# Stages of a two-block float32 network handed over token tile by token tile

## The chip, the cores and the metric

One core of a Trainium2 chip runs the whole program in one launch. The metric is device time in microseconds (us) from start to end, the median of several runs. The engines are TensorE (PE; its weight loads are listed as PEld), VectorE (DVE), ScalarE (ACT), GpSimd (POOL) and the queue engine SyncE (SP). Each engine works through its own instruction list in order and waits on semaphores that others raise.

## The reference

A first block (attention mixer and mixture of experts, two layers) feeds a second block, to which the change belongs. Its input x is 256 tokens by 1024 channels, float32, two layers deep:

```
for l in range(2):
    h = rms_norm(x, norm_pre[l, 0])
    x = x + 0.5 * rms_norm((silu(h @ w_gate) * (h @ w_up)) @ w_down, norm_post[l, 0])   # hidden width 2816
    h = rms_norm(x, norm_pre[l, 1])
    m = hybrid_mixer(h, ...)    # input product, three branches, merged = sum(gates * branch @ w_branch), m = merged @ w_out
    x = x + rms_norm(m, norm_post[l, 1])
    h = rms_norm(x, norm_pre[l, 2])
    x = x + 0.5 * rms_norm(swiglu_ffn(h, ...), norm_post[l, 2])
```

rms_norm divides each token's row by the root of its mean square over 1024 channels and multiplies by a gain row.

## The kernel before

Tokens lie on partitions in two tiles of 128 (`TT = 2`, index `tt`); `x` stays in SBUF. A product needs its left side transposed, so `h` is turned by PE in groups of four 128x128 blocks into one of two PSUM banks `t_bank` (`pe_xt`, L518). Float32 products are made from three matmuls (`mm3`, L477 to L479) of a high and a low part: ACT copies the transposed group into `xt_hi` (L525), DVE subtracts to get `xt_lo` (L533).

Weights stream through a ring of three units of 128x2048 numbers (`RING = 3`), worked in half units: SP loads a half into `w_raw`, ACT rounds it to `w_hi` (L461, `split_hi`), DVE makes `w_lo` (L466, `split_lo`), PE uses it for 12 matmuls and raises `w_used`. `ahead(u, k)` on ACT and DVE splits two halves that lie five halves (`AHEAD = 5`) in front. A half can be split only when PE has used the half six places earlier; that is what orders the splits on ACT and DVE between their other work. A unit of a 1024-wide product with 512 columns is 4 of the 8 contraction blocks, so a 512-column result takes two units and 48 matmuls for both token tiles.

A feed-forward (`feed_forward`) is 11 groups of 256 hidden columns: `gate_up` (two units into `s_bank`), SiLU on ACT (L1041), the product on DVE (L2011), the transposes of the hidden tile on PE (`hid_t`, L1471), then `down` (one unit into the four banks `g_bank`), always one group behind `gate_up`. A hardware loop over groups 2 to 10 covers most of it; the two layers are a hardware loop (`Fori(0, DEPTH)`) on every engine.

At each of five borders between stages (feed-forward to mixer, mixer to feed-forward, feed-forward to feed-forward across the layers) the work stands in a row for both tiles at once: PE ends the last product; ACT squares the four banks (L1024); DVE multiplies them by the gain (L1990), makes the variances, waits for ACT's root (L1029), adds both tiles to `x` (`norm_out`, L1997), multiplies by the next gain (`norm_in`, L1969); PE turns both tiles (L518), ACT and DVE split them, and one raise of `xt_ready` (L538) lets PE start the next stage's first unit. The next norm's own root (`in_root`, L1011 to L1017) is applied later, as a scale on the results. In the mixer the same happens between `merged2` (DVE, L2231 to L2236) and the output product: all four column groups are turned after the last branch product, and the output product is made block by block of 512 result columns.

In a hand-over the ring is full: the splits behind it wait for PE to use weights.

## Time and profile before

| | |
|---|---|
| runs | 2732.01, 2735.28, 2737.87 us; median 2735.28 |
| span of the profiled execution | 2735.5 us |
| PE busy | 2391.6 us, 87% |
| PE weight load busy | 1941.1 us, 71% |
| DVE busy | 1779.4 us, 65% |
| ACT busy | 1408.6 us, 51% |
| DMA, one hardware queue | 52.7% of 16 engines, 181 GB/s read |
| chain that ended last | PE 74%, DVE 10%, DVE's queue 5%, ACT 5%, issue 4% |

The page gives no time around the span; the profiled execution's span lies 0.2 us from the median of the runs. Busy shares are means over the whole program. PE works nearly without a gap inside a stage, so what matters is the time between stages, read from the timeline. The second block runs from about 1236 us to the end.

### The profile page before, as it was taken

The numbers are of one execution on the slowest core, as the hardware profiler recorded it, in microseconds if no ns is written. First come the engines' busy times: TensorE is split into PE (matmuls) and PEld (weight loads), VectorE is DVE, ScalarE is ACT, GpSimd is POOL, SyncE is SP. The second block draws the span as 40 slices with busy tenths as digits, with TensorE's granted clock in tenths as the row PEclk, the third lists the DMA queues.
The fourth block names the chain that finished last, engine by engine and source line by source line (L and its number), as shares of the span: only waits on it lengthen the run. The fifth ranks groups of instructions, "written<-read, shape, count | busy, mean of one in ns | idle before, by whom it ended". The sixth has DMA issues, their size and how long they took to land.

```text
span 2735.5 us, 38958 instructions
## 1 busy us (share of the span) xinstructions
PE 2391.6 (87%) x10740; PEld 1941.1 (71%) x10740; DVE 1779.4 (65%) x2346; ACT 1408.6 (51%) x1809; POOL 217.5 (8%) x290
## 2 busy tenths in 40 slices
PE   6887799988887899988998978799889989787998
PEld 5776688876765688866886756678768867566786
DVE  3756688885756688884555876645545558765455
ACT  4543477763542577754445554344444455544444
POOL 0000000000000000000001930000000029300000
PEclk9989899998988899998999978899989989888999
DMA  6433499983423599974555433445545544334552
GB/s 201 144 98 130 146 344 344 344 315 108 138 94 123 191 341 337 347 274 143 187 183 154 134 115 101 146 151 187 170 146 185 184 146 142 106 108 131 162 186 90
DMA packets 277316, 497.34 MB, mean 182 GB/s; under 512 B 20432, under 2 KB 112640, under 8 KB 277168
## 3 DMA queue, kind: packets, MB, share of 16 engines
q1 hardware_dynamic: 273264, 482.92, 52.7%
q0 software_dynamic: 3904, 12.70, 1.5%
q8 instruction: 62, 1.02, 0.2%
q14 instruction: 86, 0.70, 0.1%
HBM read 494.50 MB, written 1.05 MB: 181 GB/s over the span
## 4 chain that ended last, share of the span: by engine, by line
PE 74%; DVE 10%; DVEq 5%; ACT 5%; issue 4%; DMA 1%; ACTq 1%; SPq 0%; POOLq 0%
PE g_bank L477 14%; PE g_bank L479 14%; PE g_bank L478 14%; PE s_bank L477 8%; PE s_bank L478 8%; PE s_bank L479 8%; DVE w_lo L466 2%; PE t_bank L518 1%; PE t_bank L1359 1%; DVE conv_y L2064 1%; DVE xt_lo L533 1%; DVEq L2058 1%; DMA w_raw<-in_w_in_dram 1%; PE t_bank L1471 1%; ACT xt_hi L525 1%
## 5 line engine op out<-in xcount | busy, mean ns | idle before, releaser
L466 DVE TENSOR_TENSOR w_lo<-w_raw,w_hi 128x1024 fp32r<-128x1024 f32 x929 | 1120.0, 1230 | 563.8 <-ACT w_hi L461 543.2
L461 ACT ACTIVATE w_hi<-w_raw 128x1024 fp32r<-128x1024 f32 x929 | 971.5, 1059 | 653.3 <-PE g_bank L479 338.6
L477 PE MATMUL g_bank<-w_hi,xt_hi 128*128 128x512 f32 (+1 forms) x1088 | 450.0, 414 | 25.6 <-DVEq L538 20.5
L478 PE MATMUL g_bank<-w_lo,xt_hi 128*128 128x512 f32 (+1 forms) x1088 | 439.0, 403 | 0.0
L479 PE MATMUL g_bank<-w_hi,xt_lo 128*128 128x512 f32 (+1 forms) x1088 | 438.0, 403 | 0.0
L477 PE MATMUL s_bank<-w_hi,xt_hi 128*128 128x512 f32 x704 | 285.5, 406 | 7.0 <-DVEq L538 7.0
L478 PE MATMUL s_bank<-w_lo,xt_hi 128*128 128x512 f32 x704 | 280.9, 399 | 0.0
L479 PE MATMUL s_bank<-w_hi,xt_lo 128*128 128x512 f32 x704 | 280.4, 398 | 0.0
L477 PEld LDWEIGHTS g_bank<-w_hi,xt_hi 128*128 128x128 f32 x1088 | 218.0, 200 | 77.7 <-issue 25.6
L479 PEld LDWEIGHTS g_bank<-w_hi,xt_lo 128*128 128x128 f32 x1088 | 215.8, 198 | 47.1
L478 PEld LDWEIGHTS g_bank<-w_lo,xt_hi 128*128 128x128 f32 x1088 | 217.8, 200 | 43.5
L477 PE MATMUL g_bank<-w_hi,xg_hi 128*128 128x512 f32 x512 | 205.9, 402 | 4.7 <-issue 4.7
L479 PE MATMUL g_bank<-w_hi,xg_lo 128*128 128x512 f32 x512 | 202.4, 395 | 0.0
L478 PE MATMUL g_bank<-w_lo,xg_hi 128*128 128x512 f32 x512 | 202.4, 395 | 0.0
L477 PEld LDWEIGHTS s_bank<-w_hi,xt_hi 128*128 128x128 f32 x704 | 136.6, 194 | 36.0 <-issue 8.4
L479 PEld LDWEIGHTS s_bank<-w_hi,xt_lo 128*128 128x128 f32 x704 | 136.1, 193 | 29.5
L478 PEld LDWEIGHTS s_bank<-w_lo,xt_hi 128*128 128x128 f32 x704 | 136.5, 194 | 27.6
L477 PE MATMUL g_bank<-w_hi,ffn_t_hi 128*128 128x512 f32 x352 | 139.8, 397 | 4.8 <-DVEq L2023 4.8
L479 PE MATMUL g_bank<-w_hi,ffn_t_lo 128*128 128x512 f32 x352 | 139.7, 397 | 0.0
L478 PE MATMUL g_bank<-w_lo,ffn_t_hi 128*128 128x512 f32 x352 | 139.6, 396 | 0.0
L477 PEld LDWEIGHTS g_bank<-w_hi,xg_hi 128*128 128x128 f32 x512 | 96.3, 188 | 28.7 <-issue 7.3
L479 PEld LDWEIGHTS g_bank<-w_hi,xg_lo 128*128 128x128 f32 x512 | 96.3, 188 | 23.4
(329 smaller groups left out, 2749.2 us busy)
## 6 DMA issues: line engine op xcount, KB each, us to landing
w_raw<-in_w_in_dram SPq DMA_DIRECT2D x192, 512.0 KB, 4.3
w_raw<-in_moe_w_gate_dram SPq DMA_DIRECT2D x128, 512.0 KB, 5.2
w_raw<-in_moe_w_up_dram SPq DMA_DIRECT2D x128, 512.0 KB, 5.5
w_raw<-in_moe_w_down_dram SPq DMA_DIRECT2D x128, 512.0 KB, 5.2
w_raw<-in_ffn_w_gate_dram SPq DMA_DIRECT2D x176, 256.0 KB, 2.9
w_raw<-in_ffn_w_up_dram SPq DMA_DIRECT2D x176, 256.0 KB, 3.1
w_raw<-in_ffn_w_down_dram SPq DMA_DIRECT2D x88, 512.0 KB, 3.3
w_raw<-in_w_branch_dram SPq DMA_DIRECT2D x40, 512.0 KB, 3.5
```

Source lines behind the costliest of these rows:

```text
L461: nc.scalar.activation(half_of(w_hi, u, h), half_of(w_raw, u, h), ACT.Copy).then_inc(hi_ready, 1)
L466: nc.vector.tensor_tensor(half_of(w_lo, u, h), half_of(w_raw, u, h), half_of(w_hi, u, h).bitcast(F32), ALU.subtract).then_inc(lo_ready, 1)
L477: nc.tensor.matmul(dst, a_hi, b_hi, start=first, stop=False)
L478: nc.tensor.matmul(dst, a_hi, b_lo, start=False, stop=False)
L479: return nc.tensor.matmul(dst, a_lo, b_hi, start=False, stop=last)
L518: last = nc.tensor.transpose(bank[:, j * P:(j + 1) * P], src[:, tt, (4 * kq + j) * P:(4 * kq + j + 1) * P], ident)
L525: nc.scalar.activation(xt_hi[:, 4 * kq:4 * kq + 4, tt * P:(tt + 1) * P], t_bank[(t + i).slot(2)][:, :].rearrange("p (a b) -> p a b", a=4), ...
L533: nc.vector.tensor_tensor(xt_lo[:, 4 * kq:4 * kq + 4, tt * P:(tt + 1) * P], t_bank[(t + i).slot(2)][:, :].rearrange("p (a b) -> p a b", a= ...
L1359: last = pe.matmul(bank[:, j * P:(j + 1) * P], x[:, tt, k * P:(k + 1) * P], onehot[:, tt, bass.ds(src, 1), :].rearrange("p a b -> p (a b)" ...
L1471: last = pe.transpose(bank[:, k * P:(k + 1) * P], ffn_hid[:, tt, k * P:(k + 1) * P], ident)
L2058: dve.drain()
L2064: dve.scalar_tensor_tensor(out=conv_y[:, ch, :], in0=src, scalar=taps[:, ch, k:k + 1], in1=conv_y[:, ch, :], op0=ALU.mult, op1=ALU.add)
```

## The change

The second block's two layers are written out on PE, ACT and DVE (`for l in range(DEPTH)`); SP and GpSimd keep their loops. `hand_over` on ACT and DVE takes the place of `out_roots` and `norm_out` and handles one token tile after the other: squares, variance, root, sum into `x`, the next gain, the transposes' high and low parts, with weight splits between. PE finishes the last product of tile 0 first (`out_ready`), then that of tile 1, and the next stage begins with `first_units`: tile 0 against both first units, then tile 1. A feed-forward's last two `down` units are interleaved by tile, and the hidden transposes have a second buffer. `merged2` is turned in two halves, the first between the last two branch products, and `w_out` is used with the contraction half outside (units 35 and 36 are the first four contraction blocks for both column blocks). ACT takes a root of a constant ahead of each norm, so that the root table is there. Layer norms of the first block go tile by tile, and the output is stored in two parts.

```diff
+    if each:
+        nc.vector.drain().then_inc(xt_ready, 1)
+if not each:
+    nc.vector.drain().then_inc(xt_ready, 1)
...
 for tt in range(TT):
     dve.tensor_scalar(dst[:, tt, :], src[:, tt, :], mean_var[:, tt, 0:1], rstd[:, tt:tt + 1],
                       ALU.subtract, ALU.mult)
-dve.drain()
-for tt in range(TT):
+    dve.drain()
     dve.tensor_tensor(dst[:, tt, :], dst[:, tt, :], gain, ALU.mult)
     dve.drain()
     dve.tensor_tensor(dst[:, tt, :], dst[:, tt, :], bias, ALU.add).then_inc(row_ready, 1)
...
+nc.scalar.activation(root_of[:, :], c("ones", 0, 1), ACT.Sqrt)
...
+for half in range(2):
+    for blk in range(2):
+        load(u + (35 + 2 * half + blk), rows(d["w_out_2"], l, 4 * half, blk * 512))
...
+for tt in range(TT):
+    if stacks == 2:
+        sp.wait_ge(row_out, tt + 1)
+    else:
+        sp.wait_ge(x_ready, 2 * DEPTH + 1)
+    sp.dma_start(out[:, tt * P:(tt + 1) * P, :].rearrange("a p n -> p (a n)"), x[:, tt, :]).then_inc(x_out, 16)
...
-with act.Fori(0, DEPTH) as l:
+for l in range(DEPTH):
...
-def out_roots(n, fills, junk, factor):
+def hand_over(i, n, u_last, fills, junk, factor, t_next, split):
+    act.activation(root_of[:, :], c("ones", 0, 1), ACT.Sqrt)
     for tt in range(TT):
+        if tt == 0:
+            act.wait_ge(out_ready, 3 * l + (i + 1))
+        else:
+            for h in range(split, 4):
+                split_hi(u_last + 1, h)
+            unit_is_used(act, u_last)
         for nb in range(2):
             act.activation(junk[:, nb * 512:(nb + 1) * 512], g_bank[fills[tt][nb].slot(4)][:, :], ACT.Square,
                            scale=DM ** -0.5 / factor, accum_out=mean_sq[:, tt, nb:nb + 1])
             act.drain().then_inc(square_ready, 1)
-    for tt in range(TT):
+        if tt and t_next is not None:
+            act_xt(t_next, 2, [(0, 0), (0, 1)])
         act.wait_ge(var_ready, At(4 + n + tt, (l, 11)).value(1, 1))
         act.activation(rstd[:, tt:tt + 1], rstd[:, tt:tt + 1], ACT.Sqrt).then_inc(rstd_ready, 1)
...
+if t_next is not None:
+    act_xt(t_next + 2, 2, [(1, 0), (1, 1)])
+split_hi(u_last + 1, 4)
...
-    ahead(u, U_FFN - 1)
-    unit_is_used(act, u + (U_FFN - 1))
-    out_roots(n + 1, ffn_fills(f), ffn_junk[:, :], 0.5)
-feed_forward(first, 0, 0, 0)
+    ahead(u, U_FFN - 4)
+    ahead(u, U_FFN - 3)
+    silu(u + (U_FFN - 3), q0 + (FB - 1))
+    split_hi(u + (U_FFN - 2), AHEAD)
+    hid_t(t + (2 + 2 * FB), 1)
+    split_hi(u + (U_FFN - 2), AHEAD + 1)
+    hand_over(i, n + 1, u + (U_FFN - 1), ffn_fills(f), ffn_junk[:, :], 0.5, t_next, 3)
...
+    if k == 4:
+        act_xt(t + (T_AFTER_MIX2 + 2), 2, MERGED[0])
+ahead(u + 35)
+act_xt(t + (T_AFTER_MIX2 + 4), 2, MERGED[1])
+ahead(u + 36)
+split_hi(u + 37, AHEAD)
+hand_over(1, 6, u + 38, mix_fills(f), mix_junk, 1.0, second["t"], 2)
...
 done = pe.snap(rho, min_val=0, max_val=4)
-with pe.Fori(0, DEPTH) as l:
+for l in range(DEPTH):
     first, mixer, second = layer2(l, done)
-    def feed_forward(at, n, w, n_xt):
+    def xt_quads(src, t, i, tt):
+        for kq in range(2):
+            pe.wait_ge(normed_ready, 12 * l + (4 * i + 2 * tt + kq + 2))
+            bank = t_wait(t + (2 * tt + kq))
+            for j in range(4):
+                last = pe.transpose(bank[:, j * P:(j + 1) * P], src[:, tt, (4 * kq + j) * P:(4 * kq + j + 1) * P], ident)
+            last.then_inc(t_ready, 1)
+    def first_units(u, src, t, i, n_xt, bank_of):
+        for tt in range(TT):
+            xt_quads(src, t, i, tt)
+            bank = bank_of(tt)
+            for half in range(2):
+                uu = u + half
+                s = uu.slot(RING)
+                pe.wait_ge(xt_ready, XT_ALL2 * l + (2 * 4 + n_xt + 2 * tt + half + 1))
+                for h in range(2):
+                    half_is_split(uu, h)
+                    for k in (2 * h, 2 * h + 1):
+                        kk = 4 * half + k
+                        last = mm3(bank, xt_hi[:, kk, tt * P:(tt + 1) * P], xt_lo[:, kk, tt * P:(tt + 1) * P],
+                                   w_hi[:, s, k * 512:(k + 1) * 512], w_lo[:, s, k * 512:(k + 1) * 512], kk == 0, kk == 7)
+                    if tt == TT - 1:
+                        last.then_inc(w_used, 1)
+    def feed_forward(at, i, w, n_xt):
...
-def down(uu, q, first_, last_):
+def down(uu, q, first_, last_, parts=((0, 0), (1, 0), (0, 1), (1, 1)), b=0):
...
-    for k in range(2):
+    for tt, k in parts:
         half_is_split(uu, k)
-        for i in range(4):
-            tt, nb = i // 2, i % 2
-            bank = g_wait(f + i) if first_ and k == 0 else g_bank[(f + i).slot(4)]
+        for nb in range(2):
+            fi = f + (2 * tt + nb)
+            bank = g_wait(fi) if first_ and k == 0 else g_bank[fi.slot(4)]
             c0 = k * DM + nb * 512
-            last = mm3(bank[:, :], ffn_t_hi[:, k, tt * P:(tt + 1) * P], ffn_t_lo[:, k, tt * P:(tt + 1) * P],
+            last = mm3(bank[:, :], ffn_t_hi[:, b, k, tt * P:(tt + 1) * P], ffn_t_lo[:, b, k, tt * P:(tt + 1) * P],
                        w_hi[:, s, c0:c0 + 512], w_lo[:, s, c0:c0 + 512], first_ and k == 0, last_ and k == 1)
-        last.then_inc(w_used, 1)
+        if tt == TT - 1:
+            last.then_inc(w_used, 1)
+    return last
 def hid_t(tj, q):
...
-feed_forward(first, 1, 0, 1)
+    d9, d10, q9, q10 = u + (U_FFN - 2), u + (U_FFN - 1), q0 + (FB - 2), q0 + (FB - 1)
+    gate_up(u + (U_FFN - 4), s0 + (FB - 1))
+    down(d9, q9, False, False, ((0, 0), (0, 1)))
+    hid_t(t + (2 + 2 * FB), q10)
+    down(d9, q9, False, False, ((1, 0),))
+    down(d10, q10, False, True, ((0, 0), (0, 1)), 1).then_inc(out_ready, 1)
+    down(d9, q9, False, False, ((1, 1),))
+    down(d10, q10, False, True, ((1, 0), (1, 1)), 1)
...
-pe_block(u + 2 * i, f + 2 * i)
+if i == 0:
+    first_units(u, mix_y, t, 1, 4, lambda tt: g_wait(f + tt)[:, :])
+else:
...
-pe.wait_ge(xt_ready, 6 * l + (2 * 4 + 4))
+pe.wait_ge(xt_ready, XT_ALL2 * l + (2 * 4 + 10))
+def merged_quads(blk):
+    pe.wait_ge(merged2_ready, 2 * l + (blk + 1))
+    for tt in range(TT):
+        bank = t_wait(t + (T_AFTER_MIX2 + 2 + 2 * blk + tt))
+        for j in range(4):
+            last = pe.transpose(bank[:, j * P:(j + 1) * P], merged2[:, tt, (4 * blk + j) * P:(4 * blk + j + 1) * P], ident)
+        last.then_inc(t_ready, 1)
...
+if blk == 1 and br == 1:
+    merged_quads(0)
...
+def out_unit(half, blk, tts):
...
+out_unit(0, 0, (0, 1))
+merged_quads(1)
+out_unit(0, 1, (0, 1))
+pe.wait_ge(xt_ready, XT_ALL2 * l + (2 * 4 + 12))
+out_unit(1, 0, (0,))
+out_unit(1, 1, (0,)).then_inc(out_ready, 1)
+out_unit(1, 0, (1,))
+out_unit(1, 1, (1,))
+feed_forward(second, 2, 1, 12)
...
-def norm_in(dst, i):
-    dve.wait_ge(pre_in, 48 * l + (16 * i + 16))
-    for tt in range(TT):
-        dve.tensor_tensor(dst[:, tt, :], x[:, tt, :], gains[:, 0, :], ALU.mult)
-        dve.drain().then_inc(normed_ready, 1)
+def norm_in(dst, layer, i, tt):
+    dve.wait_ge(pre_in, 48 * layer + (16 * i + 16))
+    dve.drain()
+    for kq in range(2):
+        cols = slice(kq * 512, (kq + 1) * 512)
+        dve.tensor_tensor(dst[:, tt, cols], x[:, tt, cols], gains[:, 0, cols], ALU.mult).then_inc(normed_ready, 1)
...
-def norm_out(dst, n, sq, i, fills, factor, times=1):
+def hand_over(i, n, sq, u_last, dst, fills, factor, times, nxt, split):
     dve.wait_ge(post_in, 48 * l + (16 * i + 16))
-    fence(dve)
     for tt in range(TT):
+        def scaled(nb):
+            cols = slice(nb * 512, (nb + 1) * 512)
+            b = fills[tt][nb].slot(4)
+            dve.tensor_tensor(dst[:, tt, cols], g_bank[b][:, :], gains[:, 1, cols], ALU.mult).then_inc(g_free[b], 1)
+        dve.wait_ge(square_ready, 15 * l + (sq + 2 * tt + 1))
+        scaled(0)
+        dve.wait_ge(square_ready, 15 * l + (sq + 2 * tt + 2))
+        dve.scalar_tensor_tensor(out=rstd[:, tt:tt + 1], in0=mean_sq[:, tt, 0:1], scalar=RMS_EPS * (times / factor) ** 2,
+                                 in1=mean_sq[:, tt, 1:2], op0=ALU.add, op1=ALU.add)
+        dve.drain()
+        dve.reciprocal(rstd[:, tt:tt + 1], rstd[:, tt:tt + 1]).then_inc(var_ready, 1)
+        scaled(1)
+        dve.drain()
+        dve.wait_ge(rstd_ready, At(4 + n + tt, (l, 11)).value(1, 1))
         for nb in range(2):
             cols = slice(nb * 512, (nb + 1) * 512)
-            b = fills[tt][nb].slot(4)
-            dve.wait_ge(square_ready, 15 * l + (sq + 2 * tt + nb + 1))
...
+            dve.scalar_tensor_tensor(out=x[:, tt, cols], in0=dst[:, tt, cols], scalar=rstd[:, tt:tt + 1], in1=x[:, tt, cols],
+                                     op0=ALU.mult, op1=ALU.add)
+        if nxt is None:
+            dve.drain().then_inc(row_out, 1)
+        if tt == TT - 1:
+            dve.drain().then_inc(x_ready, 1)
+        if nxt is not None:
+            dst_next, layer, i_next, t_next, n_xt = nxt
+            norm_in(dst_next, layer, i_next, tt)
+        if tt == 0 and split < 3:
+            split_lo(u_last + 1, 2)
+        if nxt is not None:
+            dve_xt(t_next + 2 * tt, At(16 * DEPTH + n_xt + 2 * tt, (layer, XT_LAYER2)), 2, [(tt, 0), (tt, 1)], each=True)
+        split_lo(u_last + 1, 3 + tt)
+def feed_forward(at, n, sq, i, w, nxt):
     u, f, t = at["u"], at["g"], at["t"]
-    norm_in(ffn_y, i)
-    dve_xt(t, At(16 * DEPTH + n_xt, (l, XT_LAYER2)), 2)
+    if l == 0 and w == 0:
+        for tt in range(TT):
+            norm_in(ffn_y, l, i, tt)
```

How the instructions stand on three places. First DVE at the border from the first feed-forward to the mixer, before: L1990 is the gain on the product, L1991 and L1994 the variance, L1997 the sum into `x`, L1969 the next gain (its result lies in `gate`, as the mixer's does), L533 the low parts.

```order
L1990 TENSOR_TENSOR ffn_y<-g_bank,gains 128x512
L1991 SCALAR_TENSOR_TENSOR rstd<-mean_sq 128x1
L1994 RECIPROCAL rstd<-rstd 128x1
L1996 REGISTER_ALU
L1997 SCALAR_TENSOR_TENSOR x_res<-ffn_y,rstd,x_res 128x1024
L1996 REGISTER_ALU
L1997 SCALAR_TENSOR_TENSOR x_res<-ffn_y,rstd,x_res 128x1024
L1967 REGISTER_ALU
L1969 TENSOR_TENSOR gate<-x_res,gains 128x1024 x2
L532 REGISTER_ALU
L533 TENSOR_TENSOR xt_lo<-t_bank,xt_hi 128x4x128
```

The same place in the changed kernel, one token tile (L2087, L2101, L2069 and L535 are those four steps, L468 is a weight split):

```order
L2087 TENSOR_TENSOR ffn_y<-g_bank,gains 128x512
L2092 SCALAR_TENSOR_TENSOR rstd<-mean_sq 128x1
L2095 RECIPROCAL rstd<-rstd 128x1
L2087 TENSOR_TENSOR ffn_y<-g_bank,gains 128x512
L2101 SCALAR_TENSOR_TENSOR x_res<-ffn_y,rstd,x_res 128x512 x2
L2069 TENSOR_TENSOR gate<-x_res,gains 128x512 x2
L535 TENSOR_TENSOR xt_lo<-t_bank,xt_hi 128x4x128 x2
L467 REGISTER_ALU
L468 TENSOR_TENSOR w_lo<-w_raw,w_hi 128x1024
L2087 TENSOR_TENSOR ffn_y<-g_bank,gains 128x512
L2092 SCALAR_TENSOR_TENSOR rstd<-mean_sq 128x1
```

Before, both tiles pass each step together; now tile 0 passes all steps, one weight split follows, and tile 1 begins. PE at the same border before, the end of the last `down` and the start of the mixer:

```order
L479 MATMUL g_bank<-w_hi,ffn_t_lo 128x512
L1489 REGISTER_ALU
L487 ISA
L518 MATMUL t_bank<-const,gate 128x128 x8
L1489 REGISTER_ALU
L487 ISA
L518 MATMUL t_bank<-const,gate 128x128 x8
L1490 REGISTER_ALU
L454 ISA
L483 ISA
L477 MATMUL g_bank<-w_hi,xt_hi 128x512
```

PE in the changed kernel, the end of tile 0's first product and the transposes of tile 1 (L1462; L479 to L481 are the three matmuls):

```order
L479 MATMUL g_bank<-w_hi,xt_hi 128x512
L480 MATMUL g_bank<-w_lo,xt_hi 128x512
L481 MATMUL g_bank<-w_hi,xt_lo 128x512
L489 REGISTER_ALU
L1462 MATMUL t_bank<-const,gate 128x128 x8
L479 MATMUL g_bank<-w_hi,xt_hi 128x512
```

The 16 transposes that stood together ahead of the product are now eight ahead of tile 0's matmuls and eight between those of the two tiles. Third, PE between the mixer's last branch product and the output product, before:

```order
L479 MATMUL g_bank<-w_hi,xt_lo 128x512
L487 ISA
L518 MATMUL t_bank<-const,proj 128x128 x8
L487 ISA
L518 MATMUL t_bank<-const,proj 128x128 x8
L1645 REGISTER_ALU
```

and in the changed kernel, behind the branch product of unit 33:

```order
L481 MATMUL g_bank<-w_hi,xt_lo 128x512
L489 REGISTER_ALU
L1700 MATMUL t_bank<-const,proj 128x128 x8
L456 REGISTER_ALU
L479 MATMUL g_bank<-w_hi,xt_hi 128x512
L480 MATMUL g_bank<-w_lo,xt_hi 128x512
```

Eight transposes moved ahead of the last branch unit (24 matmuls); the other eight (L1700 again) stand behind 24 matmuls of the output product.

## Rows read from the trace of the kernel before

**Rows 1.** Waits of PE: line waited for, us in total, times, longest us.

```profile
PE t_bank L518 <- DVEq L1970: 62.9, 6, 15.5
```

**Rows 2.** Timeline, first feed-forward to mixer: start, us, engine, line, operation, [idle before].

```profile
1426.82 0.39 PE L479 MATMUL s_bank<-w_hi,xt_lo 128*128 128x512 f32 x1
...
1434.47 0.49 PE L477 MATMUL g_bank<-w_hi,ffn_t_hi 128*128 128x512 f32 x1 [1.20 <-DVEq L2023]
...
1440.39 0.60 ACT L1024 ACTIVATE ffn_junk<-g_bank 128x512 f32<-128x512 f32 x1 [1.75 <-PE g_bank L479]
...
1441.13 1.48 DVE L1990 TENSOR_TENSOR ffn_y<-g_bank,gains 128x512 f32<-128x512 f32 x2 [1.24 <-ACTq L1026]
...
1443.60 1.28 ACT L1029 ACT_TABLE_LOAD   x1 [0.16 <-issue]
...
1445.13 2.48 DVE L1997 SCALAR_TENSOR_TENSOR x_res<-ffn_y,rstd,x_res 128x1024 f32<-128x1024 f32 x2 [0.64 <-ACT rstd L1029]
1447.81 2.57 DVE L1969 TENSOR_TENSOR gate<-x_res,gains 128x1024 f32<-128x1024 f32 x2 [0.20 <-issue]
...
1449.23 1.96 PE L518 MATMUL t_bank<-const,gate 128*128 128x128 f32 x8 [8.87 <-DVEq L1970]
...
1451.00 0.69 DVE L533 TENSOR_TENSOR xt_lo<-t_bank,xt_hi 128x512 fp32r<-128x512 f32 x1 [0.62 <-ACT xt_hi L525]
...
1455.40 0.50 PE L477 MATMUL g_bank<-w_hi,xt_hi 128*128 128x512 f32 x1 [1.69 <-DVEq L538]
...
1466.40 0.39 PE L477 MATMUL g_bank<-w_hi,xt_hi 128*128 128x512 f32 x1
```

**Rows 3.** Timeline, PE at the four other borders, two rows each.

```profile
1729.74 0.39 PE L479 MATMUL g_bank<-w_hi,xt_lo 128*128 128x512 f32 x1
...
1795.97 1.11 PE L1471 MATMUL t_bank<-const,ffn_hid 128*128 128x128 f32 x4 [3.36 <-DVEq L2013]
...
1962.62 0.39 PE L479 MATMUL s_bank<-w_hi,xt_lo 128*128 128x512 f32 x1
...
2175.38 0.39 PE L479 MATMUL s_bank<-w_hi,xt_lo 128*128 128x512 f32 x1
...
2216.83 0.39 PE L477 MATMUL g_bank<-w_hi,xt_hi 128*128 128x512 f32 x1
...
2477.81 0.39 PE L479 MATMUL g_bank<-w_hi,xt_lo 128*128 128x512 f32 x1
...
2543.63 1.11 PE L1471 MATMUL t_bank<-const,ffn_hid 128*128 128x128 f32 x4 [3.35 <-DVEq L2013]
```

**Rows 4.** Timeline, PE and DVE: mixer's output product, layer border, first group after it.

```profile
1739.72 0.79 PE L477 MATMUL g_bank<-w_hi,xt_hi 128*128 128x512 f32 x1 [1.69 <-DVEq L538]
...
1986.79 2.58 DVE L1969 TENSOR_TENSOR ffn_y<-x_res,gains 128x1024 f32<-128x1024 f32 x2 [3.38 <-issue]
...
2011.46 0.65 PE L1471 MATMUL t_bank<-const,ffn_hid 128*128 128x128 f32 x4 [3.37 <-DVEq L2013]
```

**Rows 5.** The page's groups of weight splits: count, busy us, mean ns.

```profile
L466 DVE TENSOR_TENSOR w_lo<-w_raw,w_hi 128x1024 fp32r<-128x1024 f32 x929 | 1120.0, 1230 | 563.8 <-ACT w_hi L461 543.2
L461 ACT ACTIVATE w_hi<-w_raw 128x1024 fp32r<-128x1024 f32 x929 | 971.5, 1059 | 653.3 <-PE g_bank L479 338.6
```

**Rows 6.** Timeline, PE in the first block, a short stop between two products.

```profile
207.52 1.25 PE L518 MATMUL t_bank<-const,rot 128*128 128x128 f32 x8 [1.83 <-DVE xt_lo L533]
210.47 0.49 PE L477 MATMUL g_bank<-w_hi,xt_hi 128*128 128x512 f32 x1 [1.70 <-DVEq L538]
```

**Rows 7.** Windows: PE, PEld, DVE, ACT, POOL busy, granted clock, DMA share, GB/s.

```profile
211.00:215.00 4.00, 4.00 (x12) 3.10 (x11) 0.71 (x1) 0.00 (x0) 0.00 (x0) 0.57 0.37 131
1526.00:1692.00 166.00, 131.94 (x597) 105.29 (x596) 121.69 (x196) 90.31 (x105) 69.45 (x91) 0.86 0.36 116
2275.00:2440.00 165.00, 130.46 (x596) 104.19 (x596) 122.49 (x198) 91.23 (x107) 70.77 (x93) 0.87 0.36 117
```

**Rows 8.** Timeline, the end of the program: the store's issue.

```profile
2731.03 0.40 SPq L780 DMA_DIRECT2D out_dram<-x_res  x1
```

131 lines of the change are left out of this document (65 added, 66 removed).

## The prediction, made before the changed kernel was run

> **What bounds the kernel now.** I read the page first: PE is busy for 87% of the span and makes 74% of the chain that ended last, so inside a stage only less PE work would help. Next the list of PE's waits. Its longest entry is the wait of the transposes for the gained input: 62.9 us in 6 stops [rows 1]. Then the timeline of each stop. The reader is to see there that PE stands still while ACT and DVE take both token tiles through the same steps.
>
> At the first border [rows 2] the last gate/up matmul starts at 1426.82, so the next may start at 1427.05; I count from there, as time 0. PE waits 1.20 for the split hidden tile, ends the products at 13.3 (ACT starts at 1440.39), idles 8.87, transposes, waits for the split, and starts the mixer at 28.35. The 48 matmuls of the first two units end at 39.35 (1466.40). The span of 2735.5 is 0.2 above the median of the runs, so I take the sum from 2735.5 and change nothing for the median.
>
> **The change: end of a feed-forward.** A matmul of `down` has a pitch of 0.2335, one of the next stage 0.229 ((1466.40 - 1455.40)/48) [rows 2]. New order on PE from 0: 12 matmuls of tile 0 (2.8), hidden transposes (0.6; 0.65 in [rows 4]), 6 matmuls (1.4), 12 matmuls (2.8). Before, the hidden transposes began after 24 matmuls, at 5.6, and the split tile was there at 7.4 (1434.47 [rows 2]), 1.8 later; now 0.6 + 1.4 = 2.0 lie between, so the wait of 1.20 goes. Tile 0's sums are complete at 7.6, and 18 matmuls (4.2) remain: tile 1 ends at 11.8 instead of 13.3.
>
> **The hand-over of tile 0.** From 7.6: 0.8 until DVE has the first square; gain 0.7 (half of 1.48); variance and reciprocal 0.5; gain 0.7; `x` 1.35 (two halves, a little over the 1.24 of one full row); 0.7 for half of the next gain (2.57 over four halves is 0.64 each); with hand-offs the first transposes start at 12.5, 4.9 after 7.6. The old path had 1449.23 - 1440.39 = 8.84 from the last matmul. ACT's root table (1.28) was loaded there between squares and root [rows 2]; now it is loaded ahead of `out_ready`, between 5.9 and 7.2, when ACT is idle. DVE idled only 0.64 for that root, so it is worth at most 0.6 and is in the 4.9. The row shows the root 1.3 after the load began. The Trainium skill (ScalarE: Activation LUTs, "What ACT_TABLE_LOAD costs") gives 1283 ns for the load and about 1380 ns more of drain; the trace agrees with the first and shows no drain here, and with the drain the old path would have held 1.4 that it did not. That changes nothing in the sum.
>
> Eight transposes take 1.96, copy and low part bring the first matmul 2.7 after the first transpose began: 15.2. At 20.7 tile 0 is through both units (24 matmuls, 5.5). PE has been idle for 0.7 and 0.8.
>
> **Tile 1.** DVE is the one that comes last. After tile 0's gain (13.1) it waits for the copies, makes two low parts (0.69 each [rows 2]) by 16.0 and one weight split (1.2 [rows 5]) by 17.2. Then the same chain: gained at 21.1. PE's transposes run 21.2 to 23.1, its 24 matmuls 23.9 to 29.3. So the border takes 29.3 instead of 39.35: **10.0 saved**. In the mixer nothing waits behind: the splits of the next four halves are done at 30.7 to 34.2, each ahead of its use (32, 34.8, 37.5). What is queued behind the waiting `hand_over` on ACT and DVE are these splits; the ring holds two halves more, and that covers 5.5 of PE's time.
>
> **The other borders.** The same border in layer 2 takes 2216.83 - 2175.38 - 0.23 = 41.2 [rows 3], since it ran partly at half clock: 11.9 saved. Before a feed-forward PE stops once more, at the first hidden transposes: 3.4 [rows 3, 4]. Now ACT comes late there. It ends tile 1's copies at 23.8, then one split, the two squares of `x`, the roots (28.4), four splits of 1.06 [rows 5] (32.4), the SiLU table and SiLU (34.6), and DVE's product: PE stands from 29.3 to 35.6. That **new wait is 6.3 instead of 3.4** and is in what follows. The layer border took 2011.46 - 1962.62 - 0.23 = 48.6 [rows 3, 4], of which 3.0 are the jump back of the layer loop (DVE idle 3.38 for "issue", 0.2 to 0.4 elsewhere [rows 4, 2]); now 35.6: 13.0 saved.
>
> **Mixer to feed-forward.** Before, from the last branch matmul to the hidden transposes: 66.0 (1729.97 to 1795.97) and 65.6 (2478.04 to 2543.63) [rows 3]. It holds 9.75 from the branch product to the output product (1729.97 to 1739.72 [rows 4]). Now: eight transposes before the last branch unit 2.0, 24 matmuls 5.5, eight transposes 2.0, 24 matmuls 5.5; the merge on DVE lies under the first 24, the split of the second half under the second 24. The other 48 matmuls go by tile: tile 0 is complete after 5.5, tile 1 after 11.0, so 5.5 are covered where the feed-forward's end covers 4.2. By the same chain the first matmul of the feed-forward comes at 14.1, the last at 28.0, the hidden transposes at 34.3. Sum 2.0 + 5.5 + 2.0 + 5.5 + 34.3 = 49.3: **16.7 and 16.3 saved**.
>
> **Small parts.** First feed-forward: the transposes of tile 0 start half a row earlier and its product 3 earlier, but the late SiLU takes nearly all of it: 0.5. Output: at the first border `x` was complete at 20.6 (1445.13 + 2.48 [rows 2]); without the next gain and the low parts tile 1's is now complete at 16.1, 4.4 saved, and of the 4.5 between the store's issue and the end of the span [rows 8] I take off 0.6 for a store of half the size. Layer norms of the first block: each DVE chain keeps its length, four drains more; 0, between -0.4 and +0.7. The other order of `w_out` moves the same bytes: 0.
>
> Sum: 10.0 + 11.9 + 13.0 + 16.7 + 16.3 + 0.5 + 5.0 = 73.4.
>
> **What to take off.** The granted clock. In a stop of idle 1.83, transposes 1.25, idle 1.70 [rows 6] the clock afterwards stood at 0.57 on average over 4 us [rows 7], mostly the 1.2 GHz level; 4 x (1 - 0.57) = 1.7 us lost. Each new border has two stops of this kind (0.7 + 1.96 + 0.8 and 0.5 + 1.96 + 0.8), so 0 to 3.4 for each of five borders. They are shorter than the row's, so I take half: 1.7 each, 8.5 in all. **73.4 - 8.5 = 64.9, 2735.5 - 64.9 = 2670.6.** The ends of the unknown: no fall anywhere and transposes at the full clock (1.25 for 1.96, ten times 0.7) give 80, 2655; every fall, and 1 us more of hand-offs per tile, give 73.4 - 17 - 10 = 46, 2689.
>
> **Rivals.** (1) *The tiles cover each other badly*: DVE takes a weight split that comes late, or ACT squares tile 1 before it copies tile 0's transposes and holds the chain. For it: both engines are in order, and the new wait of 6.3 shows that ACT is short of time there. Against it: ACT is idle for 3 us before and after the copies in the chain above. If each border gave back 5 more than I counted: 64.9 - 25 = 40, 2696. (2) *It doesn't do what it says*, because the wait only moves to the next stage's first split: all that remains is the mixer's 9.75 less 4 of transposes, twice, the loop's 3.0 and the end's 5: 20, 2716. Against it: the splits of the next stage's first five halves are already made before the border. (3) *Slower*: the written-out layers. PE's list grows from 3304 to 5186 rows, and if instructions that are met for the first time had to be waited for, as at the jump (3.0 [rows 4]), it would decide from 22 such stops of 3.0 on; with 30 it is 2670.6 + 90 = 2761. Against it: the mixer's middle, which is straight code, takes 166 and 165 us with equal busy times in the first and the second pass [rows 7], so code met for the first time costs nothing there. The Trainium skill (Runtime: NRT & Kernel Launch, "Instruction fetch mechanics") says the sequencer streams straight code ahead and stalls at a taken branch to a page that it does not hold; by it the jump goes and nothing comes, as in the sum.
>
> **How the numbers follow.** Forecast 2670.6 with its clock bounds: 78%. Rival 1: 14%. Rival 2: 4%. Rival 3: 2%. Other: 2%. The range reaches from 2653 to 2693, which takes in the bounds and most of rival 1. A measurement of this kernel tells about 0.2%, 5.5 us. Faster by more: 0.96; within: 0.02; slower: 0.02.
>
> **What will show it.** PE's stops before the transposes at the borders should be near 0.7 instead of 8.9, the sum of that wait from 62.9 to under 25 (the start of the block with 15.5 stays). Between the matmuls of tile 0 and tile 1 the transposes should show about 0.5 of idle. The stop before the first hidden transposes should be 5 to 7. No idle at the layer border. In the mixer no stop before the output product. The forecast is wrong if the stop of tile 1's transposes is over 3, if hidden transposes wait over 9, or if the clock stands at half for over 7 us at each border.

## The result, and the profile after

| | before | after |
|---|---|---|
| median of 4 runs each (lowest to highest) | 2733.65 us (2730.64 to 2737.87) | 2653.47 us (2648.35 to 2654.06) |
| profiled execution: time between first and last instruction | 2735.5 | 2651.8 |
| mean granted clock | 0.922 | 0.940 |

The ratio is 0.9704, 95% interval 0.9690 to 0.9718: 81 us faster. The forecast was 2670.6 in a range of 2653 to 2693; by the ratio (0.9704 of 2733.65) the time is 2652.7, 0.3 below that range, and the median itself is 0.5 above its low end. So the sign, the mechanism of the hand-over and the places were right; the forecast saving was 16 us too small, because of what it counted for the clock (below).

The page of the changed kernel, its waits (line waited for, us in total, times, longest) and the row of the chain:

```profile
PE 2365.7 (89%) x10740; PEld 1923.3 (73%) x10740; DVE 1780.1 (67%) x2370; ACT 1406.9 (53%) x1821; POOL 218.6 (8%) x290
...
PE 74%; DVE 9%; DVEq 5%; ACT 5%; issue 4%; ACTq 1%; DMA 1%; SPq 0%; POOLq 0%
...
PE t_bank L1612 <- ACTq L1170: 39.7, 7, 8.9
...
PE t_bank L1524 <- DVEq L2130: 20.8, 4, 5.4
PE t_bank L1462 <- DVE ffn_y L2069: 16.2, 2, 15.3
...
PE t_bank L1462 <- DVE gate L2069: 2.1, 4, 0.8
```

PE's wait for gained rows, 62.9 us before [rows 1], now stands as 16.2 in 2 stops (15.3 of it the start of the block, as before) and 2.1 in 4. The largest wait at the borders is now the one before the first hidden transposes, four stops of up to 5.4 (3.4 before). The wait at L1612 is one inside the mixers that the change doesn't touch: PE stands some 37 us within each mixer's middle before, in stops of up to 9.1, and 36 and 37 us after. That PE works nearly without a gap inside a stage holds for the feed-forwards, not for the mixers. The timeline of PE over the first border (start, us, line, [idle before]) answers [rows 2]:

```profile
1423.69 0.40 PE L481 MATMUL s_bank<-w_hi,xt_lo 128*128 128x512 f32 x1
...
1436.51 1.18 PE L1462 MATMUL t_bank<-const,gate 128*128 128x128 f32 x8 [0.78 <-DVE gate L2069]
1439.01 0.49 PE L479 MATMUL g_bank<-w_hi,xt_hi 128*128 128x512 f32 x1 [1.32 <-DVEq L540]
...
1445.01 1.18 PE L1462 MATMUL t_bank<-const,gate 128*128 128x128 f32 x8 [0.27 <-DVE gate L2069]
1447.16 0.47 PE L479 MATMUL g_bank<-w_hi,xt_hi 128*128 128x512 f32 x1 [0.98 <-issue]
...
1452.69 0.39 PE L479 MATMUL g_bank<-w_hi,xt_hi 128*128 128x512 f32 x1
```

With time 0 at 1423.92, the same point as in the forecast, tile 0's transposes start at 12.6 (forecast 12.5), its product at 15.1 (15.2), it is through at 20.8 (20.7), tile 1's transposes start at 21.1 (21.2) and the border ends at 28.77 (29.3). The eight transposes take 1.18, not 1.96. DVE's chain of tile 0; tile 1's, which the forecast had as the one that comes last, can only begin behind it:

```profile
1432.39 0.69 DVE L2087 TENSOR_TENSOR ffn_y<-g_bank,gains 128x512 f32<-128x512 f32 x1 [1.30 <-ACTq L1042]
...
1434.19 1.41 DVE L2101 SCALAR_TENSOR_TENSOR x_res<-ffn_y,rstd,x_res 128x512 f32<-128x512 f32 x2
1435.68 1.29 DVE L2069 TENSOR_TENSOR gate<-x_res,gains 128x512 f32<-128x512 f32 x2
1438.04 1.52 DVE L535 TENSOR_TENSOR xt_lo<-t_bank,xt_hi 128x512 fp32r<-128x512 f32 x2 [1.06 <-ACT xt_hi L527]
1439.76 1.23 DVE L468 TENSOR_TENSOR w_lo<-w_raw,w_hi 128x1024 fp32r<-128x1024 f32 x1 [0.21 <-issue]
1440.90 0.68 DVE L2087 TENSOR_TENSOR ffn_y<-g_bank,gains 128x512 f32<-128x512 f32 x1
```

The last row is the first step for tile 1: DVE goes from one tile to the next without a pause.

**Where the time went**, from PE's rows in both traces, with the forecast's cuts. "Middles" of the feed-forwards reach from the first hidden transposes to the last gate/up matmul, those of the mixers from the 49th matmul to the end of the branch product; the eight transposes that now stand ahead of the last branch unit (0.8) are counted with the border.

| stretch | before | forecast | after |
|---|---|---|---|
| head and block 1, to the first transposes of block 2 | 1238.2 | 1238.2 | 1235.5 |
| first feed-forward, to its hidden transposes | 22.1 | 21.6 | 22.4 |
| middles of four feed-forwards | 664.6 | 664.6 | 663.1 |
| feed-forward to mixer, twice | 39.4, 41.2 | 29.3, 29.3 | 28.8, 28.8 |
| layer border | 48.6 | 35.6 | 35.4 |
| middles of two mixers | 524.8 | 524.8 | 524.3 |
| mixer to feed-forward, twice | 66.0, 65.6 | 49.3, 49.3 | 47.2, 47.2 |
| end of the program | 25.1 | 20.1 | 19.2 |
| taken off for the clock | | +8.5 | |
| sum | 2735.5 | 2670.6 | 2651.8 |

The five borders give 73.4 instead of the forecast's 67.9 - 8.5 = 59.4. That this equals the forecast's sum of 73.4 before the clock is chance. The 2.7 of the first row are scatter: block 1 is the same code in the kernel before and in two experiments below that only touch block 2, and it ended at 1238.2, 1234.2 and 1231.2; in the changed kernel and its variants, at 1230.8 to 1238.2. So below I also give the part of the profiled span behind that point, **block 2**: 1497.3 before, 1416.4 after. Their difference, 81.0, is what the ratio says too.

### The profile page after: what moved, and what is told of

Read it like the earlier page. It is cut to its first block, busy times and chain, and to the rows that moved or that the text cites. A ratio compares the mean times of both kernels' runs of the same rounds, so it can differ in the third digit from the quotient of the medians.

```text
span 2651.8 us, 38763 instructions
## 1 busy us (share of the span) xinstructions
PE 2365.7 (89%) x10740; PEld 1923.3 (73%) x10740; DVE 1780.1 (67%) x2370; ACT 1406.9 (53%) x1821; POOL 218.6 (8%) x290
## 3 DMA queue, kind: packets, MB, share of 16 engines
q1 hardware_dynamic: 273280, 482.92, 55.1%
q8 instruction: 63, 1.03, 0.2%
## 4 chain that ended last, share of the span: by engine, by line
PE 74%; DVE 9%; DVEq 5%; ACT 5%; issue 4%; ACTq 1%; DMA 1%; SPq 0%; POOLq 0%
PE g_bank L479 14%; PE g_bank L480 14%; PE g_bank L481 14%; PE s_bank L479 8%; PE s_bank L481 8%; PE s_bank L480 8%; DVE w_lo L468 2%; PE t_bank L1385 1%; DVE conv_y L2182 1%; ACT w_hi L463 1%; DVEq L2176 1%; PE t_bank L1524 1%; DMA w_raw<-in_w_in_dram 1%; DVE xt_lo L535 1%; PE t_bank L1319 1%
## 5 line engine op out<-in xcount | busy, mean ns | idle before, releaser
L468 DVE TENSOR_TENSOR w_lo<-w_raw,w_hi 128x1024 fp32r<-128x1024 f32 x929 | 1117.1, 1229 | 494.5 <-ACT w_hi L463 472.2
L479 PE MATMUL g_bank<-w_hi,xt_hi 128*128 128x512 f32 (+1 forms) x1088 | 446.1, 410 | 23.7 <-DVEq L543 14.0
L481 PE MATMUL g_bank<-w_hi,xt_lo 128*128 128x512 f32 (+1 forms) x1088 | 435.5, 400 | 0.0
L479 PE MATMUL s_bank<-w_hi,xt_hi 128*128 128x512 f32 x704 | 284.2, 404 | 10.6 <-DVEq L540 10.6
L481 PE MATMUL s_bank<-w_hi,xt_lo 128*128 128x512 f32 x704 | 279.3, 397 | 0.0
L479 PEld LDWEIGHTS g_bank<-w_hi,xt_hi 128*128 128x128 f32 x1088 | 216.5, 199 | 74.7 <-issue 23.1
L481 PEld LDWEIGHTS g_bank<-w_hi,xt_lo 128*128 128x128 f32 x1088 | 214.0, 197 | 46.2
L479 PE MATMUL g_bank<-w_hi,xg_hi 128*128 128x512 f32 x512 | 206.2, 403 | 4.9 <-issue 4.9
L481 PE MATMUL g_bank<-w_hi,xg_lo 128*128 128x512 f32 x512 | 203.0, 396 | 0.0
L479 PEld LDWEIGHTS s_bank<-w_hi,xt_hi 128*128 128x128 f32 x704 | 135.9, 193 | 39.8 <-issue 7.6
L481 PEld LDWEIGHTS s_bank<-w_hi,xt_lo 128*128 128x128 f32 x704 | 135.0, 192 | 29.2
L479 PE MATMUL g_bank<-w_hi,ffn_t_hi 128*128 128x512 f32 x352 | 139.7, 397 | 0.0
L481 PE MATMUL g_bank<-w_hi,ffn_t_lo 128*128 128x512 f32 x352 | 138.9, 395 | 0.0
L479 PEld LDWEIGHTS g_bank<-w_hi,xg_hi 128*128 128x128 f32 x512 | 96.4, 188 | 29.2 <-issue 7.5
L481 PEld LDWEIGHTS g_bank<-w_hi,xg_lo 128*128 128x128 f32 x512 | 96.4, 188 | 23.5
```

What stands on the lines that cost most here:

```text
L468: nc.vector.tensor_tensor(half_of(w_lo, u, h), half_of(w_raw, u, h), half_of(w_hi, u, h).bitcast(F32), ALU.subtract).then_inc(lo_ready, 1)
L479: nc.tensor.matmul(dst, a_hi, b_hi, start=first, stop=False)
L481: return nc.tensor.matmul(dst, a_lo, b_hi, start=False, stop=last)
```

## Experiments

| kernel | median | ratio to before, interval | block 2 |
|---|---|---|---|
| changed kernel | 2653.5 | 0.9704 (0.9690, 0.9718) | 1416.4 |
| b_layers | 2713.9 | 0.9933 (0.9917, 0.9950) | 1477.9 |
| b_preload | 2722.6 | 0.9959 (0.9945, 0.9973) | 1485.1 |
| a_late | 2686.0 | 0.9831 (0.9815, 0.9848) | 1451.3 |
| a_merged | 2668.8 | 0.9766 (0.9750, 0.9782) | 1432.9 |
| a_slow1 | 2655.4 | 0.9720 (0.9703, 0.9736) | 1417.3 |
| a_slow3 | 2676.7 | 0.9793 (0.9776, 0.9809) | 1437.0 |
| a_noload | 2655.2 | 0.9717 (0.9702, 0.9731) | 1417.4 |
| a_fill | 2641.7 | 0.9668 (0.9652, 0.9684) | 1408.8 |
| c_root | 2646.9 | 0.9681 (0.9665, 0.9697) | 1409.4 |
| c_tile | 2647.5 | 0.9683 (0.9666, 0.9699) | 1414.8 |
| c_swap | 2650.4 | 0.9696 (0.9682, 0.9711) | 1415.8 |
| c_all | 2648.7 | 0.9687 (0.9671, 0.9703) | 1410.1 |
| c_fill | 2640.7 | 0.9656 (0.9642, 0.9670) | 1402.2 |
| c_fill2 | 2640.5 | 0.9657 (0.9644, 0.9671) | 1403.2 |

b_ kernels start from the kernel before, a_ and c_ from the changed one. "0.001 of ratio" is 2.7 us.

### What the forecast priced at 3: the layers written out (b_layers, b_preload)

```diff
-            with act.Fori(0, DEPTH) as l:
+            for l in range(DEPTH):
```

(the same on PE and DVE, block 2 alone.)

> The kernel before, with the two layers of block 2 written out on PE, ACT and DVE instead of looped; nothing else. Theory A (the forecast's): the jump back goes, 3.0 us at the layer border (DVE idle 3.38 there against 0.2 to 0.4 elsewhere), all other stages as before: 2735.5 - 3.0 = 2732.5. Theory B: the written-out layers also carry the 10 us that the changed kernel saved outside its borders (first block 2.7, end 0.9 more than forecast, stages between the borders the rest): then the mixer's middle and the feed-forwards' middles get shorter here too, and the time is 2722 to 2728. Theory C (rival 3 of the forecast): code met for the first time is waited for: the second layer's stages get longer than in the kernel before, over 2738.

It gave 18, with an interval of 14 to 23, in a part that I had put at 3.0; by block 2's part 19.5, of which the first feed-forward gave 3.1 and the layer border 7.6. The jump is there as forecast: PE's stop at the layer border goes from 12.11 to 8.69, 3.4. What I had not expected stands before each first hidden transposes. ACT (start, us, line, operation, [idle before]) in the kernel before, then in b_layers, at the same place, the first SiLU of the second feed-forward:

```profile
1789.93 1.06 ACT L461 ACTIVATE w_hi<-w_raw 128x1024 fp32r<-128x1024 f32 x1 [1.66 <-PE s_bank L479]
1792.72 1.28 ACT L1041 ACT_TABLE_LOAD   x1 [1.72 <-PE s_bank L479]
1794.01 0.84 ACT L1041 ACTIVATE ffn_silu<-s_bank,rstd_in 128x256 f32<-128x256 f32 x2
```

```profile
1778.99 1.06 ACT L461 ACTIVATE w_hi<-w_raw 128x1024 fp32r<-128x1024 f32 x1 [1.66 <-PE s_bank L479]
1780.07 1.28 ACT L1041 ACT_TABLE_LOAD   x1
1781.71 0.84 ACT L1041 ACTIVATE ffn_silu<-s_bank,rstd_in 128x256 f32<-128x256 f32 x2 [0.36 <-PE s_bank L479]
```

In the loop ACT waits 1.72 for PE's sums and loads the SiLU table after that wait. Written out, it loads the table first and waits only with the SiLU. (The wait's value is in a register in the loop and a constant in the written-out code; that this is why the load changes sides is argued, the rows show only that it does.) PE's stop behind it:

```profile
1783.64 0.82 PE L1471 MATMUL t_bank<-const,ffn_hid 128*128 128x128 f32 x4 [1.97 <-DVEq L2013]
```

It was 3.36 [rows 3]; 1.4 less, in each of four feed-forwards. The second gain is the clock behind the stop. Over about the 8 us from the first hidden transposes, in the kernel before and in b_layers (columns as in [rows 7]):

```profile
1260.00:1268.00 8.00, 7.69 (x25) 6.30 (x26) 2.79 (x5) 2.77 (x4) 0.00 (x0) 0.64 0.19 67
```

```profile
1254.00:1262.00 8.00, 8.00 (x37) 6.63 (x36) 4.43 (x5) 3.43 (x5) 0.00 (x0) 1.00 0.43 130
```

That feed-forward's middle took 166.7 before and 164.1 here. So theory A is out, C too (the second layer's mixer takes 271.0 in both, from the 49th matmul to the output product). B has the direction, but not the size: 2713.9 lies below its 2722 to 2728. Whether the table load alone does it, without any layer written out:

```diff
                     ahead(u, 1)
+                    act.activation(ffn_junk[:, 0:1], c("ones", 0, 1), ACT.Silu)
                     silu(u + 1, q0)
```

> The kernel before, looped as it was, with one SiLU of a single column between the second pair of weight splits and the first SiLU of each feed-forward, so that ACT loads the SiLU table (1.28 us) before it waits for the gate/up sums and not behind that wait. Theory B1 (the written-out layers gained because a wait on a constant rides on the SiLU itself and lets the table load go ahead of it): the stop before the first hidden transposes goes from 3.4 to 2.0 in all four feed-forwards, as in the kernel with the layers written out; 5.6 us, and 2 to 6 more where the clock no longer falls behind the shorter stop: 2722 to 2728. Theory B2 (it was the number of register instructions): the table load moves, but the stop stays over 3, and the time is within 2 of before.

B1 came out: stops of 2.08 to 2.09 in all four, block 2 shorter by 12.2, ratio 11 us (7 to 15). The rest of b_layers is the jump's 3.4 and about 4 in products that ran at a higher clock in that trace, which I can't tell from scatter. The Trainium skill (ScalarE: Activation LUTs, "What ACT_TABLE_LOAD costs") calls the load an instruction of its own, 1283 ns. The rows agree, and these rows show the load on either side of a wait. Of its further 1380 ns of drain no row here shows anything; in b_preload the column's activation starts 1.29 after the load began.

In the changed kernel this gain isn't there. Its ACT comes late at the same place, and the load is on the path though no wait stands before it:

```profile
1954.48 3.90 ACT L463 ACTIVATE w_hi<-w_raw 128x1024 fp32r<-128x1024 f32 x4
1958.40 1.28 ACT L1062 ACT_TABLE_LOAD   x1
1959.69 0.84 ACT L1062 ACTIVATE ffn_silu<-s_bank,rstd_in 128x256 f32<-128x256 f32 x2
```

So b_layers' 18 don't add to the hand-over's gain. What the changed kernel would do with its layers looped wasn't run; that of them it keeps only the jump is argued from these rows.

### What the tiles' overlap and the mixer's new order are worth (a_late, a_merged)

```diff
                             act.wait_ge(out_ready, 3 * l + (i + 1))
+                            unit_is_used(act, u_last)
```

> The changed kernel, but token tile 0 is not handed over before tile 1's matmuls of the last unit are done too: ACT waits for the whole unit before tile 0's first square. Theory A: DVE's chain of the two tiles is serial and sets the border, so each border gets longer by all that lay under it: 18 matmuls (4.2 us) at three feed-forward borders and at the end of the program, 24 (5.5) at two mixer borders: 16.8 + 11.0 = 27.8, so 2653.5 + 28 = 2681, and 3 to 8 more if the clock falls in the stops of about 5 us that come before tile 0's transposes. Theory B (most of the gain is from the row being taken in halves and tiles, not from the cover): under 12 more, 2665 or less.

33 more by the medians, 35 by block 2's part: theory A with its clock. Feed-forward borders +5.7, +6.9 and +4.6, mixer borders +5.7 twice, end +4.2. PE now stops 5 us before tile 0's transposes, they run at half and so does the product:

```profile
1955.31 1.96 PE L1463 MATMUL t_bank<-const,ffn_y 128*128 128x128 f32 x8 [5.09 <-DVE ffn_y L2070]
1957.95 0.79 PE L479 MATMUL s_bank<-w_hi,xt_hi 128*128 128x512 f32 x1 [0.68 <-DVEq L540]
```

```diff
-                        if blk == 1 and br == 1:
-                            merged_quads(0)
...
+                merged_quads(0)
+                merged_quads(1)
+                pe.wait_ge(xt_ready, XT_ALL2 * l + (2 * 4 + 12))
                 out_unit(0, 0, (0, 1))
-                merged_quads(1)
...
```

(and the copies and low parts on ACT and DVE likewise.)

> The changed kernel, but all 16 transposes of the merged row stand behind the last branch unit again, on PE, ACT and DVE; the output product keeps its new order. Theory A: the 9.75 us between branch product and output product come back, and 1.6 for the transposes inside the products go: 8.2 for each of two mixers, 16.3: 2670. Theory B (that place was hidden otherwise, and the mixer's borders gain by the token tiles alone): under 6 in all, under 2660.

15.3 more by the medians, 16.5 by block 2's part, against 16.3 expected. The two mixer borders went from 47.2 to 55.1, 7.9 each where 8.2 was expected (1.0 of it came back because the clock held behind the stop of 2.30 in this trace). So the mixer's 9.75 was priced about right, and it falls to 1.6 and not to the forecast's 4: inside a running product eight transposes cost 0.79, at the full clock (the changed kernel, ahead of the last branch unit):

```profile
1707.98 1.03 PE L1700 MATMUL t_bank<-const,proj 128*128 128x128 f32 x8
1708.77 0.48 PE L479 MATMUL g_bank<-w_hi,xt_hi 128*128 128x512 f32 x1
```

### What a longer chain and a longer stop cost (a_slow1, a_slow3, a_noload)

```diff
...
+                            for _ in range(1):   # a_slow3: range(3)
+                                dve.tensor_tensor(dst_next[:, tt, 0:512], x[:, tt, 0:512], gains[:, 0, 0:512], ALU.mult)
+                                dve.drain()
```

> The changed kernel, but DVE computes the first half of each next gain twice, in each of the five hand-overs and for each tile: 0.65 us and a drain, 0.7, ten times. Theory A (DVE's chain sets the border, and the clock holds): tile 0's transposes come 0.7 later and tile 1's 1.4 later, 1.4 for each of five borders: 7, so 2660.5; the stop before tile 0's transposes goes from 0.8 to 1.5. Theory B (the clock was kept only by stops that happened to be short): the same, and the clock falls in the feed-forward borders too, 1.7 for each: 2669. Theory C (DVE has slack of more than 0.7 per tile): under 3.

> The changed kernel, with the first half of each next gain computed four times instead of once: 2.1 us more of DVE for each tile (the run with 0.7 gave +1.8, +0.6 and +1.6 at the three feed-forward borders and nothing at the two mixer borders). Theory A (chain alone, clock holds): 4.2 at each feed-forward border, 0 to 2.8 at the mixer ones: 13 to 18 more, 2666 to 2671. Theory B (the clock was kept because the stop before tile 0's transposes was 0.8; at 2.9 it falls): 1.7 more for each of five borders, 2674 to 2680, with the eight transposes at 1.96 instead of 1.1 and a granted clock under 0.9 over the border.

a_slow1: the three feed-forward borders got longer by 1.8, 1.6 and 0.6, the mixer borders by nothing; the median rose by 2.0, the ratio by 4. So theory A's 7 was too much. What covers the longer chain at the last three of these borders is PE's own product at half clock: there the changed kernel's tile 1 transposes already began 1.2 us after DVE had their first half ready, where 0.13 is usual (the rows stand below, where the clock term is answered). a_slow3: +4.6, +4.5, +3.7, and 2.5 at each mixer border, 17.7 in borders, 20.6 in block 2, 24 by the ratios. The three feed-forward borders and the transposes at 1.18 follow theory A, but the time, 2676.7, lies above A's 2666 to 2671 and in B's 2674 to 2680; and the clock did fall, as B had it:

```profile
1441.95 1.18 PE L1462 MATMUL t_bank<-const,gate 128*128 128x128 f32 x8 [3.13 <-DVE gate L2069]
1444.24 0.79 PE L479 MATMUL g_bank<-w_hi,xt_hi 128*128 128x512 f32 x1 [1.11 <-DVEq L540]
```

```profile
1443.00:1451.00 8.00, 6.89 (x20) 5.34 (x19) 6.88 (x12) 0.97 (x3) 0.00 (x0) 0.57 0.22 66
```

The second fence is the window behind the stop, at 0.57. The border lost nearly nothing to it (4.6 against 4.2 of DVE): tile 1's transposes start at 1452.61, 0.82 after DVE began their gain at 1451.79, as at the same border of the changed kernel, and tile 0's slow product ends just in time. Both were missing in the forecast's clock term: whether the clock falls, and how much of the slowed work somebody waits for.

```diff
-                    act.activation(root_of[:, :], c("ones", 0, 1), ACT.Sqrt)
```

> The changed kernel without the early loading of the root table in the hand-overs: the table is then loaded for tile 0's root, behind its squares. Theory A (the forecast's price): DVE idles for the root by at most 0.6 at each of five borders and the end: 2 to 3.6 more, 2656 to 2657. Theory B (the whole load is on the path): 1.28 six times, 7.7, 2661. Theory C (hidden under DVE's gain of 0.67): within 1.

DVE's idle before `x` is 0.57, the forecast's 0.6 to the row; the time rose by 1.7 in medians, 3.6 by the ratios, 1.0 in block 2. That sides with A and leaves C (within 1) possible; B is out.

```profile
1435.93 1.41 DVE L2100 SCALAR_TENSOR_TENSOR x_res<-ffn_y,rstd,x_res 128x512 f32<-128x512 f32 x2 [0.57 <-ACT rstd L1045]
```

### The new wait of 5.4, and the clock behind it (a_fill, c_root, c_fill)

```diff
                     pe.sem_inc(s_ready, 1)
+                    spare = g_wait(f)
+                    for _ in range(20):
+                        pe.matmul(spare[:, :], xt_hi[:, 7, P:2 * P], xt_hi[:, 0:2, :].rearrange(...), start=True, stop=True)
                     hid_t(t + 4, q0)
```

> The changed kernel, with 20 matmuls of 512 columns whose result is thrown away, in PE's stop of 4.6 to 5.4 us before the first hidden transposes of each feed-forward (20 x 0.229 = 4.6). Nothing else moves. Theory A (the clock falls because PE stands still there): clock 0.73, 0.76 and 0.74 over the 9 us after that stop goes to 1.0, 1.3 to 1.8 us less for each of four: 2653.5 - 6 = 2647.5. Theory B (the fall has another cause, or the added matmuls end later than the hidden tile is ready): 2653 or more.

Work that nobody needs makes the kernel 10 us faster by the ratios, 7.6 in block 2. No chain got shorter; the mixer borders take 46.4 from the end of the branch product to the hidden transposes in both. Behind the stop, in the changed kernel and in a_fill:

```profile
1961.00:1970.00 9.00, 8.38 (x31) 6.92 (x32) 3.76 (x6) 3.10 (x5) 0.00 (x0) 0.74 0.68 218
```

```profile
1954.00:1963.00 9.00, 8.14 (x38) 6.82 (x39) 4.78 (x7) 3.73 (x5) 0.00 (x0) 1.00 0.73 245
```

38 matmuls and transposes fall into it where 31 did. The four middles go from 166.0, 165.5, 165.8 and 165.8 to 163.9 each.

c_root shortens the chain instead: ACT makes the squares of `x` in its idle time inside the hand-over and loads the SiLU table before the four splits.

```diff
+                        if tt and nxt is not None:
+                            in_square(0, junk)
                         act.wait_ge(var_ready, At(4 + n + tt, (l, 11)).value(1, 1))
                         act.activation(rstd[:, tt:tt + 1], ...ACT.Sqrt).then_inc(rstd_ready, 1)
+                    if nxt is not None:
+                        in_square(1, junk)
+                        ...
+                        act.activation(rstd_in[:, :], rstd_in[:, :], ACT.Sqrt)
                     if t_next is not None:
                         act_xt(t_next + 2, 2, [(1, 0), (1, 1)])
                     split_hi(u_last + 1, 4)
+                    if nxt is not None:
+                        act.activation(root_of[:, :], c("ones", 0, 1), ACT.Silu)
```

> The changed kernel with ACT's work before a following feed-forward in another order: the squares of x and their root are made inside the hand-over, in ACT's idle time before the copies of tile 0 and 1 (3.4 and 4.6 us), and the SiLU table is loaded right behind the first split after them. Theory A (ACT's queue makes the stop of 5.4 before the first hidden transposes: 2.5 of squares, 0.9 of roots, 1.3 of table load): the SiLU starts with the end of the gate/up product, the stop falls to 2.0 at three of four feed-forwards, 10 us, and 3 to 5 more from the clock behind it: 2639 to 2643. Theory B (DVE's splits, or the next weights, take its place): the stop stays over 4, 2648 or more.

The stop fell to 2.94, 1.97 and 2.94 and block 2 by 7.0, the borders by 2.3 to 2.5 each. ACT's SiLU starts at 1958.78 after 0.30 of waiting for PE, so its queue is off the path at the layer border. The clock didn't come back as hoped: the two middles behind the mixers took 166.7, against 165.5 and 165.8 in the changed kernel. Are the two gains one?

```diff
+                    for _ in range(18 if l == 0 and w == 0 else 10 if w else 6):
```

> The kernel with the roots inside the hand-over, and thrown-away matmuls of 512 columns in what is left of the stop before the first hidden transposes: 18 (4.1 us) in the first feed-forward, 10 (2.3) behind a mixer, 6 (1.4) at the layer border. Theory A (a shorter stop and a stop in which PE stays busy are separate gains: about 2.4 us each at three borders from the roots, and 1.7 to 2.2 of half clock behind each of four stops): 2653.5 - 7 - 8 = 2638, below both the run with 20 thrown-away matmuls (2641.7) and that with the roots (2646.9). Theory B (the run with 20 had its gain from the clock only, and a stop filled or shortened gives the same microseconds once): no better than 2641.7.

By block 2 they are two: it is 14.2 shorter than the changed kernel's, 7.6 + 7.0 expected, and c_fill2, which is the same kernel with seven matmuls more, gives 13.2. The whole times don't settle it: 2640.7 against a_fill's 2641.7 by the medians (theory A had 2638), 0.9656 against 0.9668 by the ratios, with intervals that overlap. c_fill and c_fill2 are the fastest of all, 13 us below the changed kernel by the ratios.

### Four that gave nothing (c_tile, c_swap, c_all, c_fill2)

All four contain c_root's change. c_tile puts `silu_first`, `hidden_first` and the transposes of tile 0 ahead of tile 1's in the first block run; c_swap also moves one line on DVE; c_all adds matmuls in the remaining stop to both.

```diff
+                    silu_first(q0)
                     ahead(u)
                     ahead(u, 1)
-                    silu(u + 1, q0)
+                    silu(u + 1, q0, (1,))
```

> The kernel with the roots inside the hand-over (stops of 2.9, 2.0 and 2.9 before the first hidden transposes at three feed-forwards, 4.5 at the first), and now the SiLU, the product and the hidden transposes of tile 0 of the first block run as soon as tile 0's gate/up sums are there, ahead of tile 1's. Theory A (what is left of the stop is ACT's and DVE's work on two tiles behind the last product, 0.84 + 0.87 and hand-offs): it falls by 0.42 + 0.43, 0.8 to 1.2 each, and the clock holds behind it at more of them, 1.2 each: 2646.9 - 4 to 8 = 2639 to 2643. Theory B (ACT's in-order queue is now held by the wait for tile 0 and splits come later): 2645 or more.

```diff
-                        if tt == 0 and split < 3:
-                            split_lo(u_last + 1, 2)
                         if nxt is not None:
                             dve_xt(...)
+                        if tt == 0 and split < 3:
+                            split_lo(u_last + 1, 2)
```

> The kernel before this one, and at the two mixer-to-feed-forward borders DVE makes tile 0's low parts before the third half's split and not behind it. Theory A (that split, 1.23, makes the stop of 2.30 before the first product of tile 0): the stop goes to 1.1 at both borders, and the half clock behind it (1.8 at one) goes too: 2.4 to 5 less than the run with tile 0's SiLU. Theory B (DVE's chain of tile 1 sets the border whatever stands between): the stop moves to tile 1's transposes, under 1 in all.

> Both changes, and matmuls of 512 columns whose result is thrown away in what is left of the stop before the first hidden transposes: 14 (3.2 us) at the first feed-forward, 5 (1.1) at the others. Theory A (each idle stretch of 2 to 5 us costs up to 1.8 of half clock behind it, and 20 such matmuls gave 1.7 to 2.2 at each of four): 2 to 7 less than without them, near 2633 to 2637. Theory B (stops this short no longer lower the clock): the same as without, or 1 to 2 more where the added matmuls end after the hidden tile is ready.

In c_tile the stop became two, and PE needs both:

```profile
1759.83 0.44 PE L1554 MATMUL t_bank<-const,ffn_hid 128*128 128x128 f32 x2 [0.91 <-DVEq L2165]
1762.71 0.69 PE L1554 MATMUL t_bank<-const,ffn_hid 128*128 128x128 f32 x2 [2.45 <-DVEq L2172]
```

Theory B for all three. In c_swap the stop of 2.30 before tile 0's product stayed (2.31), so that split isn't its cause. The changed kernel's rows at this border name another:

```profile
1737.20 0.60 ACT L1040 ACTIVATE proj<-g_bank 128x512 f32<-128x512 f32 x1 [1.32 <-PE g_bank L481]
1737.99 0.60 ACT L1040 ACTIVATE proj<-g_bank 128x512 f32<-128x512 f32 x1
1738.84 1.08 ACT L527 ACTIVATE xt_hi<-t_bank 128x512 fp32r<-128x512 f32 x2 [0.17 <-issue]
1739.47 1.52 DVE L535 TENSOR_TENSOR xt_lo<-t_bank,xt_hi 128x512 fp32r<-128x512 f32 x2 [1.17 <-ACT xt_hi L527]
```

PE turns tile 0 from 1737.00 on, but ACT first squares tile 1, whose sums have just come, and copies tile 0's transposes only at 1738.84; in c_swap DVE waits 2.30 for these copies. So the stop is the order of ACT's list. No run has the copies first. c_all's matmuls stand before tile 0's transposes, and the 2.45 of the layer border is as it was behind them; its block 2 is 5 shorter than c_tile's, its ratio isn't.

```diff
+                        for _ in range(7 if tile_fill and tt == 0 else 0):
+                            pe.matmul(bank, xt_hi[:, 8, P:2 * P], xt_hi[:, 8:10, :].rearrange(...), start=True, stop=True)
```

> The same, and seven more thrown-away matmuls (1.6 us) in the stop of 2.30 between tile 0's transposes and its first product, at the two mixer-to-feed-forward borders. Theory A (a stop of 2.30 is long enough to lower the clock: in one of the two borders of the changed kernel the first eight matmuls behind it ran at half, 1.8 us): 0 to 3.6 less than the run without them. Theory B (the clock behind that stop is as it is for another reason): no difference.

The mixer borders changed from 43.9 to 43.7: theory B. The clock did hold behind the filled stop, and tile 1's transposes came 9.45 us after tile 0's instead of 10.50. But with c_root's order ACT makes the squares and roots of `x` before it copies tile 1's transposes, and it began these copies 1.46 after the transposes instead of 0.64. So this run says that the fall costs little in c_root's order; the changed kernel's ACT waits 4.58 for these transposes, and there it costs more, as the next section shows.

## Why the prediction was off

**Right, step by step.** The chain of tile 0 (12.5 forecast, 12.6 measured), the serial chain of tile 1 on DVE, the layer border (35.6, 35.4; this one holds 1.0 of clock, see below), the feed-forward borders (29.3, 28.8), the vanished stop before the output product, the root table's 0.6 (0.57), the end's `x` at 16.1 after the last gate/up matmul (2647.28 + 1.41 - 2632.59 = 16.1), the late SiLU that takes the first feed-forward's gain. The new wait was announced as 6.3 and is 5.4 (4.6 in the first feed-forward). Rival 1 (bad cover) came in part and without its price: at the mixer borders ACT does square tile 1 before it copies tile 0's transposes, which makes the stop of 2.30, but tile 1's transposes idle 0.27 at most and no border is longer than forecast. Rival 2 fell with the trace and with a_late, rival 3 with b_layers: written-out layers cost nothing and gave 18.

**Wrong: "1.7 each, 8.5 in all".** This is the term that failed, and its twin, the 1.96 for eight transposes. I took the clock after one short stop [rows 6, 7] as what half of ten new stops would do. In the changed kernel it fell behind one stop at three of the five borders: both mixer borders and the layer border. The row behind the first of these stops, then the windows over all three (columns as in [rows 7]):

```profile
1737.00 1.03 PE L1462 MATMUL t_bank<-const,ffn_y 128*128 128x128 f32 x8
1740.34 0.79 PE L479 MATMUL s_bank<-w_hi,xt_hi 128*128 128x512 f32 x1 [2.30 <-DVEq L540]
1740.92 0.63 PE L480 MATMUL s_bank<-w_lo,xt_hi 128*128 128x512 f32 x1
```

```profile
1740.00:1745.00 5.00, 4.66 (x13) 3.75 (x14) 4.48 (x9) 0.20 (x1) 0.00 (x0) 0.66 0.46 150
1941.00:1946.00 5.00, 4.75 (x14) 3.78 (x15) 4.48 (x9) 0.20 (x1) 0.00 (x0) 0.66 0.19 63
2446.00:2451.00 5.00, 4.56 (x13) 3.64 (x14) 4.48 (x9) 0.23 (x2) 0.00 (x0) 0.66 0.46 153
```

In each about eight matmuls ran at half: 8 x (0.43 - 0.23) = 1.6 of PE's work. About 1.0 of it is in the time. At the layer border tile 1's transposes wait for the slow product, and ACT for them:

```profile
1946.53 1.29 DVE L2069 TENSOR_TENSOR ffn_y<-x_res,gains 128x512 f32<-128x512 f32 x2 [0.18 <-issue]
1948.42 1.03 PE L1462 MATMUL t_bank<-const,ffn_y 128*128 128x128 f32 x8
1949.05 1.08 ACT L527 ACTIVATE xt_hi<-t_bank 128x512 fp32r<-128x512 f32 x2 [4.57 <-PE t_bank L1462]
```

With the clock at 1.00 the same transposes come 0.8 after DVE began their gain and not 1.9, as in a_fill, whose layer border takes 34.4 instead of 35.4; a_merged's takes 34.4 too. Behind the same stop of 2.30 a_merged's mixer borders kept the clock, and from the product to the hidden transposes they take 19.4 instead of 20.4. So the clock costs the five borders about 2.9 in place of 8.5: it fell behind three of the ten stops, and of each fall 0.6 lay under DVE's chain. The two borders from feed-forward to mixer had no fall, as over the whole first one:

```profile
1423.00:1452.00 29.00, 25.65 (x118) 20.08 (x117) 18.86 (x31) 15.86 (x31) 2.34 (x5) 1.00 0.42 117
```

The transposes ran at the full clock at all five: 1.03 to 1.18 for eight. The forecast had both at their full-clock value in its bound of 2655, and took the middle because one row spoke for a fall. Ahead of that row PE had stopped 1.83 and 1.70 around 1.25 of transposes; here it stops 0.8 and 1.3 around 1.2. The runs put more beside it:

| stop before the transposes | eight transposes | behind them |
|---|---|---|
| none, then 2.3 before the product (changed kernel, mixer borders) | 1.0 | 0.66 over 5 us |
| 0.8 to 0.9, then 1.2 to 1.3 (changed kernel, three borders) | 1.1 to 1.2 | 1.00 twice, 0.66 over 5 us once |
| 3.1 (a_slow3) | 1.18 | 0.57 over 8 us |
| 5.0 (a_late) | 1.96 | 0.79 for the first matmul: half |
| 8.9 (before, [rows 2]) | 1.96 | 0.50 or 0.79 |

The length of the stop alone doesn't decide it. The first border, with the same instructions and the same stops of 0.8 and 1.3, kept the clock in three traces (28.8 us long: changed kernel, a_merged, c_root) and lost it in six (29.9: a_fill and the other c_ kernels). In a_fill:

```profile
1432.00:1437.00 5.00, 4.43 (x12) 3.50 (x13) 4.48 (x9) 0.25 (x2) 0.00 (x0) 0.66 0.20 45
```

So 1.0 to 1.1 a border is the price of a fall, and whether it comes at such a stop was partly luck; what decides it stays open.

**Wrong by size.** From 2670.6 to the profiled 2651.8 are 18.8: 14.0 in the five borders, of which 5.6 are the clock term (2.9 for 8.5) and 8.4 their other terms, most of these the transposes at full clock (at the mixer borders two groups of merged transposes were counted at 2.0 each and cost 0.8); 0.9 at the end; 2.0 in the middles, less 0.8 at the first feed-forward; and the 2.7 of the first row, which are scatter. The transposes' shorter time shows only in part at the other borders: tile 0's product starts at 15.1, as forecast, since it waits for its low part, 1.3 instead of 0.8. The range missed by less than a microsecond, since I built its low end from the same terms and left nothing below.

**Missed, without a price here.** The table load behind the wait [rows 4, the stop of 3.37]: I read that stop as ACT's and DVE's work, and didn't ask why a load with nothing before it starts only after the wait. It was worth 11 us in the kernel before.

## What to carry to other kernels

Handing a row over in pieces pays what lies under the first piece, here 4.2 to 5.5 us a border, and it pays twice when it keeps PE's stops short: price every stop with the clock that rows show behind it, and then ask how much of the slowed work someone waits for. Read the clock over the whole stretch and not by the first matmul: at two of the three borders where it fell, the first matmul still took 0.49. Look at each table load that follows an idle time: if its ACT waited for data first, load the table ahead with a one-column activation. Where a stop can't be shortened, thrown-away matmuls in it are worth a try.

## What the runs showed of the hardware

- ACT's table load (1.28 us, in every row) stands behind the wait in the looped code and ahead of it in the written-out one: 1.4 us of PE's stop per feed-forward.
- PE at rest costs more than the rest: after a stop of 5.4 the granted clock of the next 9 us was 0.74, with 20 useless matmuls in the stop it was 1.00, 1.7 to 2.2 us a time.
- Behind the same stops of 0.8 and 1.3 around eight transposes the clock fell in six traces (0.66 over 5 us) and stayed at 1.00 in three: 29.9 against 28.8 us for the border.
- Half the clock behind a stop costs little where another engine's chain is longer (a_slow3: 0.57 over 8 us, 0.4 lost; changed kernel: 1.6 us of slower matmuls, 1.0 lost).
- The first block, the same code in all variants of a kernel, took 1230.8 to 1238.2 in profiled executions; two whole spans can differ by 7 us there, so a difference between two traces says something only when it is taken from a stretch.
